# Three adaption rows of a transformer kernel turned into columns by small transfers on SyncE's queue

## The reference

```
def second_block(x, c, w_ada, b_ada, norm_g, ...):
    c_act = jax.nn.silu(c)
    for layer in range(DEPTH):
        ada = jnp.einsum('bd,de->be', c_act, w_ada[layer]) + b_ada[layer]
        shift, scale, gate = jnp.split(ada, 3, axis=-1)
        h = rms_norm(x, norm_g[layer]) * (1.0 + scale[:, None, :]) + shift[:, None, :]
        y = even_mixer(h, ...) if layer % 2 == 0 else odd_mixer(h, ...)
        x = x + gate[:, None, :] * y
    return rms_norm(x, final_g)
```

## Time and profile before

| | us |
|---|---|
| median of 3 runs | 1542.48 (1540.66 to 1543.0) |
| the profiled execution | 1541.35 |
| its span | 1539.5 |
| PE busy | 1519.2 |
| PEld busy | 1347.7 |
| DVE busy | 1031.6 |
| ACT busy | 431.5 |

### The profile page before, as it was taken

How to read it: one execution, slowest core, us unless ns; L and a number is a source line. 1 busy time by engine, 2 the same in 40 slices (tenths; PEclk the granted TensorE clock), 3 DMA queues, 4 the chain that set the end, 5 groups by cost and what they waited for, 6 DMA issues and landing times.

```text
span 1539.5 us, 27730 instructions
## 1 busy us (share of the span) xinstructions
PE 1519.2 (99%) x11151; PEld 1347.7 (88%) x11151; DVE 1031.6 (67%) x1932; ACT 431.5 (28%) x925; POOL 12.4 (1%) x26
## 2 busy tenths in 40 slices
PE   8999999999999999999999999999999999999998
PEld 7998869898899999899878899799999787678887
DVE  5788886477667774678897467667775565545663
ACT  5415424012100001335423201300001456424431
POOL 1000000000000000100000000000000000000000
PEclk9999999999999999999999999999999999999999
DMA  8543453353475455344242442485454745553320
GB/s 275 187 165 112 149 153 111 111 203 125 143 241 164 152 168 178 116 164 155 101 159 91 163 147 87 150 274 165 158 178 159 251 156 219 211 203 119 132 103 28
DMA packets 172385, 243.40 MB, mean 158 GB/s; under 512 B 16830, under 2 KB 95332, under 8 KB 172260
## 3 DMA queue, kind: packets, MB, share of 16 engines
q1 hardware_dynamic: 170372, 237.96, 45.1%
q10 hardware_dynamic: 1888, 3.67, 0.7%
HBM read 240.56 MB, written 1.05 MB: 157 GB/s over the span
## 4 chain that ended last, share of the span: by engine, by line
PE 95%; DVE 3%; ACT 1%; issue 1%; DMA 0%; SPq 0%; DVEq 0%; POOL 0%; ACTq 0%
PE psum L631 34%; PE psum L1646 27%; PE psum L1501 7%; PE psum L1301 3%; PE psum L3113 3%; PE psum L445 2%; PE psum L1560 2%; PE psum L1296 2%; PE psum L3205 2%; PE psum L428 1%; PE psum L1430 1%; PE psum L3213 1%; PE psum L461 1%; PE psum L665 1%; PE psum L1402 1%; PE psum L1341 1%
## 5 line engine op out<-in xcount | busy, mean ns | idle before, releaser
L631 PE MATMUL psum<-hT,ring 128*128 128x256 f32 x1552 | 342.8, 380 | 1.1 <-DVE hT L1974 0.9
L631 PEld LDWEIGHTS psum<-hT,ring 128*128 128x128 f32 x1552 | 292.3, 190 | 45.5 <-issue 7.1
L631 PE MATMUL psum<-uT,ring 128*128 128x256 f32 x384 | 84.9, 380 | 0.0
L1646 PE MATMUL psum<-hT,ring 128*128 128x128 f32 x704 | 82.4, 275 | 1.0 <-issue 1.0
L631 PEld LDWEIGHTS psum<-uT,ring 128*128 128x128 f32 x384 | 72.6, 190 | 10.4 <-DVE uT L1164 0.6
L1646 PEld LDWEIGHTS psum<-hT,ring 128*128 128x128 f32 x704 | 80.4, 192 | 1.5 <-issue 1.5
L1927 ACT ACTIVATE SCR<-SCR 128x512 f32<-128x512 f32 x22 | 13.9, 631 | 219.9 <-DVEq L2711 219.9
L512 DVE TENSOR_TENSOR psum<-psum,const 128x512 f32<-128x512 f32 (+4 forms) x41 | 22.1, 559 | 62.4 <-PE psum L445 61.6
L491 ACT ACTIVATE SCR<-psum,stats 128x128 f32<-128x128 f32 (+2 forms) x128 | 49.9, 406 | 25.6 <-DVE stats L526 24.8
L1646 PE MATMUL psum<-G,ring 128*128 128x128 f32 x400 | 47.8, 276 | 0.0
L1922 ACT ACTIVATE SCR<-psum 128x256 f32<-128x256 f32 (+1 forms) x30 | 10.7, 356 | 127.8 <-PE psum L1646 127.8
(11 more groups left out here) (651 smaller groups left out, 3003.9 us busy)
## 6 DMA issues: line engine op xcount, KB each, us to landing
ring<-in_w_in SPq DMA_DIRECT2D x46, 1024.0 KB, 7.0
ring<-in_ffn_w_gate_up SPq DMA_DIRECT2D x88, 512.0 KB, 5.7
ring<-in_w_ada SPq DMA_DIRECT2D x24, 1024.0 KB, 8.0
ring<-in_ffn_w_down SPq DMA_DIRECT2D x16, 1024.0 KB, 6.1
ring<-in_w_in_odd SPq DMA_DIRECT2D x16, 1024.0 KB, 7.4
ring<-in_w_in_even SPq DMA_DIRECT2D x10, 1024.0 KB, 7.1
ring<-in_x_w_kv SPq DMA_DIRECT2D x8, 1024.0 KB, 5.8
ring<-in_ssm_w_glu SPq DMA_DIRECT2D x8, 1024.0 KB, 6.2
```

Source lines behind the costliest of these rows:

```text
L631: ins = nc.tensor.matmul(b[0:width, n * S:n * S + S], w[k // 4][:, k % 4, c0[n]:c0[n] + width], tile(k), start=k == 0, stop=k == kt - 1)
L1646: ins = nc.tensor.matmul(banks[job][:, at:at + P], left, right, start=first, stop=last)
```

## The change

The three jobs `ada11 turned`, `ada12 turned` and `ada13 turned` are gone from TensorE's list, and with them the three sums that VectorE made from PSUM. In their place SP issues 16 transfers for each part: each takes 128 neighbouring numbers of one strip's row, all in one partition, and writes them as one column of the new tile `ada_cols`, one number in each of 128 partitions. The transfers of parts 1 and 2 are issued ahead of the first load of `ada14`, those of part 3 ahead of the first load of `q0`; SP waits first until ScalarE has copied those rows. VectorE waits for all 48 after the second step of the even residual, then adds strips and bias for the three parts and makes the gains. The semaphore `pool_step`, which nothing used, is dropped. The core of the diff:

```
+def ada_moved_store(V, link, m, layer, n, nth):
+    cols = m["ada_cols"][:, 16 * nth:16 * nth + 16].rearrange("p (s i) -> p i s", s=4)
+    link(V.tensor_reduce(m["ada_sum"], cols, AXX, ALU.add))
+    at = ROWS["b_ada"][0] + 4 * n
+    link(V.tensor_tensor(m["ada"][:, 24 * layer + 4 * n:24 * layer + 4 * n + 4], m["ada_sum"],
+                         m["par"][layer][:, at:at + 4], ALU.add))
...
-           14: ["ada13"], 16: ["part 0", "part ada11"], 17: ["part 1"],
-           18: ["part 2", "part ada12", "part ada13"]}
+           14: ["ada13"], 16: ["part 0"], 17: ["part 1"], 18: ["part 2"]}
...
+ADA_MOVED = [1, 2, 3]
...
-SECOND_O += ["b heads0", "b heads1", "b heads2", "b heads3", "ada11 turned", "ada12 turned", "ada13 turned", "square 2"]
+SECOND_O += ["b heads0", "b heads1", "b heads2", "b heads3", "square 2"]
...
-            if i == 16:
-                ada_store(V, dve, link, m, ojobs, 1, 1)
-            if i == 18:
-                ada_store(V, dve, link, m, ojobs, 1, 2)
-                ada_store(V, dve, link, m, ojobs, 1, 3)
+        def moved_parts(c):
+            if c == 1:
+                dve.wait_ge(sig["ada_moved"], 16 * 16 * len(ADA_MOVED))
+                for nth, n in enumerate(ADA_MOVED):
+                    ada_moved_store(V, link, m, 1, n, nth)
                 gains(1)
+
         dve.wait_ge(sig["x_normed"], KT)
-        residual("even out", 0, 4, EVEN_TILES)
+        residual("even out", 0, 4, EVEN_TILES, moved_parts)
...
+        def ada_moved(*parts):
+            for n in parts:
+                second_jobs.evacuated(sp, f"ada1{n}")
+            for n in parts:
+                row = m["ada_rows"][(6 + n) % ADA_SLOTS]
+                for strip, i in itertools.product(range(4), range(4)):
+                    at = 16 * ADA_MOVED.index(n) + 4 * strip + i
+                    put(m["ada_cols"][:, at:at + 1], row[32 * strip:32 * strip + 1, i * P:(i + 1) * P],
+                        second["ada_moved"])
...
-        ring.load(sp, {"0 hq.0": masks_in, "0 kv.0": tables_in, "0 glu gate.0": next_layer, "2 qb.0": small_params},
+        ring.load(sp, {"0 hq.0": masks_in, "0 kv.0": tables_in, "0 glu gate.0": next_layer, "2 qb.0": small_params,
+                       "2 ada14.0": lambda: ada_moved(1, 2), "2 q0.0": lambda: ada_moved(3)},
                   FIRST_PIECES, summed)
...
+        m["ada_cols"] = sb("ada_cols", [P, 48])
```

More of the change, by code:

```diff
@@ L949, in first_block_layer @@
     o_done = shared["o_done"]
-    dve_step, act_step, pool_step = (shared[n] for n in ("dve_step", "act_step", "pool_step"))
+    dve_step, act_step = (shared[n] for n in ("dve_step", "act_step"))
     negmax_ready, rows_ready = shared["negmax_ready"], shared["rows_ready"]
@@ L3134, in ab_fill @@
                     ada(1, int(name[4]))
-                elif name.startswith("part ada"):
-                    ada_turned(1, int(name[9]))
                 elif name.startswith("part"):
@@ L3693, in _, with load_weights @@
                                          ALU.mult), f"final{n}")
-def load_weights(nc, block, a, m, sems, ring):
+def load_weights(nc, block, a, m, sems, ring, second_jobs):
     first, second = sems["named"][0], sems["named"][DEPTH]
@@ L3820, in build @@
         pe_done, o_done = sem("jobs_done"), sem("out_jobs_done")
-        steps = {f"{n}_step": (sem(f"{n}_step"), [0]) for n in ("dve", "act", "pool")}
+        steps = {f"{n}_step": (sem(f"{n}_step"), [0]) for n in ("dve", "act")}
         sems = {"shared": dict(steps, o_done=o_done, negmax_ready=sem("negmax_ready"), rows_ready=sem("rows_ready"),
@@ L3838, in build @@
         with nc.Block() as block:
-            load_weights(nc, block, a, m, sems, ring)
+            load_weights(nc, block, a, m, sems, ring, books[DEPTH][0])
             for layer in range(DEPTH):
```

## The result

| | before | after |
|---|---|---|
| median, 7 runs each | 1541.98 (1540.66 to 1543.0) | 1546.76 (1546.56 to 1546.9) |
| the profiled execution, its span | 1541.35, 1539.5 | 1546.56, 1544.7 |

The ratio is 1.0032, with a 95% interval of 1.0023 to 1.0041: the change costs 4.8 us. The forecast was +0.6. The two profiled spans differ by 5.2 us.

The account below looks back on a forecast made before the run. The prediction took TensorE, busy 99% of the span, as the bound. Removed transposes, -1.41 us, plus late columns, +2.0, made +0.6 us, so a median of 1543.1 us, with a range of 1540.3 to 1560.

Parts of the forecast that it names:

- The gain: TensorE, output projection: three groups of four transposes leave its queue, -1.41 us.
- The step on SP: SP's queue: each small transfer takes 0.64 us, by the dearer flag transfer, out of 0.47 to 0.64.
- Rival B: VectorE's wait: columns come early at a 0.47 us step, all 1.41 us stay, 1541.1 us; chance 0.12.
- A: SP's queue: issues are dearer and SP becomes the bound from 0.70 us per step; 1551 at 0.80; chance 0.42.
- Rival C: SP's 48 transfers do not overlap, each taking 2.2 us in turn: +72.6 us, about 1615; chance 0.03.
- D: TensorE loses the transposes but waits elsewhere in the same stretch: no change, 1542.5 us; chance 0.05.
- The first thirty-two: SP, ahead of the four loads: 32 issues from 1331.1 take 20.5 us, until 1351.6.
- The last sixteen: SP, behind the four loads: last issue at 1365, last column at 1367, 2.0 us too late.
- What a late column costs: VectorE between second and third residual: columns cost nothing until 1365.0, then each microsecond costs one; TensorE waits at the square sum.
- The covers: TensorE's loads: parts 4 and 5 covered by 9 us; the odd block's second half lands at 1374.3, needed at 1377.8.
- third sign of being wrong: TensorE: the prediction is wrong if the loads behind the small transfers are what TensorE waits for.
- the likeliest case: Whole kernel: a step of 0.47 to 0.70 us, Rival B and D included, -1.4 to +3.5 us; chance 0.52.

Follow-up runs that it names:

- experiment 1: The change without the 48 transfers and their wait, columns read as zeros; 0.9989 of the kernel before, -1.7 us.
- experiment 8: The change with part 2's sixteen transfers issued a second time ahead of the loads, VectorE waiting for all 64; 1.0104 of the kernel before, +16.0 us.
- experiment 2: The kernel before, transposes kept, plus the 48 transfers, read by nobody and waited for only after the odd layer's tiles; 1.0008, +1.2 us.
- experiment 4: The change with VectorE's wait for the columns after the fourth residual step instead of the second; 1.0011 of the kernel before, +1.7 us.
- experiment 6: The change with only parts 1 and 2 moved by transfers, part 3 transposed as before; 0.9991 of the kernel before, -1.4 us.
- experiment 3: The change with all 48 transfers ahead of the four loads of the last two parts; 1.0064 of the kernel before, +9.9 us.
- experiment 5: The change with one transfer of 512 numbers per strip, twelve in all, ScalarE's copy reordering the row; 0.9988 of the kernel before, -1.9 us.
- experiment 7: The change with part 3's sixteen transfers issued on ScalarE's queue instead of SP's; 0.9992 of the kernel before, -1.2 us.
- experiment 9: The change with one transfer per strip, the row's order made in TensorE's product and ScalarE's copy plain; 1.0021 of the kernel before, +3.2 us.

## Why the prediction was right and wrong

- *The gain*, -1.41: right. The rows give -1.31, and experiment 1 -1.7 with an interval of 0.3 to 3.1. The stretch read as free of waits has one, of 0.28 us ahead of the last transposes at 1376.76; it is there in both kernels and changes no sum.
- *The step on SP*, 0.64 by the dearer flag: right to the last digit, 10.26 us for sixteen that stand free. Rival B's 0.47 is out, and so is A's condition, a step above 0.70. Rival C is out too: the transfers overlap, some 2.1 us each from issue to landing where the queue is free, but 0.64 apart. D is out: TensorE lost the transposes and waited at the foretold place.
- *The first thirty-two*, put at 20.5 us: 22.07. Of the first sixteen, issues of 1.24, 0.78 and 1.10 us were held: the first two while the four loads of the projection's weights were landing (until 1338.25), the third behind that (see the last section). The start was 0.16 us earlier than counted, the four loads' issue took 0.47 longer: the last sixteen began 1.9 us late.
- *The last sixteen*, **the step that failed**: "I put the last issue at 1365, at the pace at which the loads drain". That allowed them 1365 - 1353.7 = 11.3 us, 1.1 of it held; they took 14.63. The hold ended when it was put, at 1365.04, but in part by luck: the loads began 1.4 us later than counted, and the fourth landed at 1367.3, not at 1364.6. And the sixteen do not all go out as the loads end. A held queue lets them through one by one: eight went through in 9.5 us, and the other eight then cost their full 0.64 each. The hold is added to SP's time; I had treated the two as running side by side. So the last issue ended at 1370.21, and the last column came at 1371.66 instead of 1367. The 4.7 us between are nearly the error of the forecast (+4.8 against +0.6). Without the holds, 1.46 us in the first sixteen and 4.37 in the last, the last column would by these rows have come at about 1365.8, near the end of the free time (1365.6 by the next point).
- *What a late column costs*: the place was right (VectorE between the second and third residual, TensorE at the square sum), and so was the slope of one (experiment 8). The free time ends a little later than 1365.0: the bound was set by the start of the fourth residual, while TensorE needs its square only at L612. At full clock L612 could have begun right behind that square, at about 1377.4, instead of 1371.3 (1368.47 + 1.85 for L665 + 0.97 for L609): 6.1 us for columns at 1371.69, so they were free until 1365.6.
- *The clock*: not in the sum at all. Of the 6.93 us 6.1 are the wait by this reckoning, and the other 0.8 are products at 1.2 GHz.
- *The covers*: that of the loads for parts 4 and 5 held. "Covered" for the odd layer's loads was right for 1366 and false for the 1370.25 that came: their way, put at 8.3 us, was 8.05, so their second half came at 1378.3, and the need at 1377.8 was met only since TensorE was later still. Experiments 2 and 4, without TensorE's wait for the columns, show it as 1 and 3 us. So the third sign of being wrong, TensorE waiting for the loads behind the small transfers, stands right behind the wait that was foretold.
- *The chances*: the outcome, +0.3%, lies among the slower cases, which had 0.45, and within the range. But it came neither by A's dear issue nor as the likeliest case: what A described at its place happened at the free step's price, by the hold (holds included, the 48 took 0.77 us each).

## What to carry to other kernels

Count a small transfer by its issue: here, from one partition to 128, it took SP 0.64 us from one to the next, whether it moved 128 or 512 numbers, so pack as many numbers into one as the layouts allow. An issue behind megabytes on its own queue is held, and what is still to be issued comes on top of the hold; put small urgent transfers ahead of the loads as far as the loads can spare the time (experiment 6, and experiment 3 for the limit), or on another engine's queue. After each wait that is found, look for the one behind it, since a load that seems covered may be covered only by that wait.

## What the hardware showed that was not expected

- A tiny transfer is held as well as a large one: up to 2.07 us for an issue of 512 B behind four loads of 1 MB, 14.2 to 14.8 us for sixteen in four kernels, against 10.3 free and 10.5 on ScalarE's queue (six of them beside the loads). What SP counts there (pieces, bytes or transfers) was not tried.
- Not every long issue stands behind loads. In experiment 3 one took 1.75 us when only small transfers were under way, and at that moment, from 1361.16, a transfer that the profile calls "instruction" ran on another queue (SP's issue; then the kind, with number, MB and share of the 16 engines' time from 1360.5 to 1361.7):

```profile
1361.13 1.75 SPq L3714 DMA_DIRECT2D ada_cols<-bT  x1
...
q8 instruction: 1, 0.02, 6.9%
```

  Experiment 8 has the same, 1.46 us at 1358.82. In the change the issues of 1.10 us at 1338.98 and of 1.36 at 1361.77 coincide with such a transfer, so up to 1.3 of its 5.8 us of holds may belong to it and not to the loads. That it is the cause is not shown.
- The granted clock fell not only after the long stands. In the profile of experiment 1 it fell after two short gaps, of 0.77 and 1.11 us, which the kernel before has too, at full clock (0.77 and 1.13 us, from 1334.8 to 1337.5). The windows of experiment 1, same columns, and then one of the kernel before:

```profile
1334.00:1337.00 3.00, 1.67 (x18) 1.16 (x14) 2.86 (x15) 2.83 (x11) 0.00 (x0) 0.92 1.05 410
1337.00:1342.00 5.00, 4.45 (x18) 3.53 (x19) 2.10 (x9) 2.02 (x11) 0.00 (x0) 0.50 1.05 401
1342.00:1345.00 3.00, 3.00 (x12) 2.48 (x11) 0.00 (x0) 0.00 (x0) 0.00 (x0) 0.78 1.05 406
...
1337.00:1342.00 5.00, 4.48 (x28) 3.91 (x29) 2.07 (x9) 2.00 (x11) 0.00 (x0) 1.00 1.05 405
```

  It cost that execution about 3 us (it took 1542.86 us, the median of its kernel is 1539.87). The profiles of experiments 3, 5 and 7 have the same fall at this place, those of 2, 4, 6 and 8 don't. The same can be read from the runs of the kernel before on that chip: with a granted clock of 0.999 over the span they took 1540.6 to 1542.2 us, with 0.998 1541.9 to 1543.4, and the one with 0.996 1544.2. Gains of 1 to 2 us have to be read across this, so a single execution does not tell them.
- Steps inside a row cost about twice: ScalarE's copy that writes numbers 16 B apart takes 1.12 instead of 0.61 us (experiment 5), and TensorE's product that reads them 512 B apart 3.92 instead of 1.92 (experiment 9). The Trainium skill ("SBUF — State Buffer", section "Door 1: The DMA port swizzle") says that accesses run at full rate as long as they fall in the same line of 16 B, and that each that crosses to a new line pays a penalty; the trace agrees in direction, and gives a factor of about two for these two.
